# Moving sixteen modulation slabs of the first block and twelve of the last layer to other stages

## The reference, cut to what matters

```python
def ada(c, w, b):                      # first block: w_ada (1024 x 6144), for c and for c_ctx
    m = jax.nn.silu(c) @ w + b
    return split(m, 6)                 # sh1, sc1, g1, sh2, sc2, g2

u_lat = modulate(x, sh1, sc1) @ w_in   # layer norm, then * (1 + sc1) + sh1
mix   = token_mixer(u_lat, ...)        # state-space part, Fourier part, pooling part, @ w_out
x     = post_norm(x, mix, g1, ...)
x     = post_norm(x, conv_ffn(modulate(x, sh2, sc2), ...), g2, ...)

# second block, two layers, ada_w_2[layer] (1024 x 6144)
mod = silu(c) @ ada_w[layer] + ada_b[layer]          # six vectors of 1024
# layer 0: mLSTM heads and banded window attention, then a squared-ReLU MLP
# layer 1: full attention, then a squared-ReLU MLP
```

## Time and profile before

| | us |
|---|---|
| median of 3 runs | 2562.12 (2561.9 to 2563.28) |
| the profiled execution's own time | 2555.24 |
| its span | 2553.4 |
| TensorE busy | 2366.8 (93%) |
| GpSimd busy | 1061.9 (42%) |
| VectorE busy | 1166.3 (46%) |
| ScalarE busy | 792.8 (31%) |

### The profile page before, as it was taken

One profiled execution on the slowest core, in us unless ns is written; L12 is line 12 of the kernel. 1 busy time (PEld: TensorE's weight loads), 2 busy tenths in 40 slices (PEclk: granted clock), 3 DMA queues, 4 the chain that ended last, 5 costly groups with the idle time before them and its releaser, 6 DMA issues. The chain is left out here.

```text
span 2553.4 us, 35025 instructions
## 1 busy us (share of the span) xinstructions
PE 2366.8 (93%) x14323; PEld 1921.2 (75%) x14323; DVE 1166.3 (46%) x1938; ACT 792.8 (31%) x1301; POOL 1061.9 (42%) x728
## 2 busy tenths in 40 slices
PE   6987688999997999978989999999989999899999
PEld 5866466777775789866768888888867688688887
DVE  4417647856563680478345142322327752411111
ACT  4232433333334422245232111111124353322221
POOL 3326234655553332324236243443434124656553
PEclk8998898999998999979989999999989999899999
DMA  8570213544442112100113233333311101233321
GB/s 273 165 231 1 69 62 111 163 136 157 145 161 76 33 50 67 34 1 2 40 43 116 66 116 124 109 127 105 114 44 50 50 1 50 83 99 99 99 83 50
DMA packets 224701, 229.95 MB, mean 90 GB/s; under 512 B 7375, under 2 KB 221219, under 8 KB 224547
## 3 DMA queue, kind: packets, MB, share of 16 engines
q1 hardware_dynamic: 224211, 227.66, 27.7%
q10 hardware_dynamic: 336, 0.11, 0.0%
HBM read 225.65 MB, written 2.10 MB: 89 GB/s over the span
## 5 line engine op out<-in xcount | busy, mean ns | idle before, releaser
L1271 POOL TENSOR_TENSOR w_lo<-ring,w_hi 128x1024 fp32r<-128x1024 f32 x126 | 306.1, 2432 | 374.3 <-ACT w_hi L1265 374.3
L2087 DVE SCALAR_TENSOR_TENSOR xT<-ps,mods,xT 128x512 f32<-128x512 f32 (+1 forms) x160 | 108.5, 684 | 555.4 <-PE ps L1333 519.5
L1265 ACT ACTIVATE w_hi<-ring 128x1024 fp32r<-128x1024 f32 x126 | 132.7, 1057 | 537.8 <-PE ps L1333 510.4
L1331 PE MATMUL ps<-hidden_hi,w_hi 128*128 128x512 f32 (+1 forms) x768 | 273.3, 356 | 0.0
L1332 PE MATMUL ps<-hidden_lo,w_hi 128*128 128x512 f32 (+1 forms) x768 | 272.0, 354 | 0.0
L1333 PE MATMUL ps<-hidden_hi,w_lo 128*128 128x512 f32 (+1 forms) x768 | 271.6, 354 | 0.0
L2373 DVE SCALAR_TENSOR_TENSOR ffn_sums<-ps,cols,ffn_sums 128x441 f32<-128x441 f32 (+2 forms) x352 | 215.0, 687 | 105.7 <-ACT ffn_sums L2294 105.7
L1331 PE MATMUL ps<-h_hi,w_hi 128*128 128x512 f32 (+1 forms) x688 | 245.4, 357 | 1.6 <-issue 1.6
L1332 PE MATMUL ps<-h_lo,w_hi 128*128 128x512 f32 (+1 forms) x688 | 244.2, 355 | 0.0
L1333 PE MATMUL ps<-h_hi,w_lo 128*128 128x512 f32 (+1 forms) x688 | 243.8, 354 | 0.0
L2317 POOL TENSOR_TENSOR ffn_w_lo<-ring,ffn_w_hi 128x1024 fp32r<-128x1024 f32 (+2 forms) x76 | 161.6, 2128 | 194.2 <-ACT ffn_w_hi L2270 194.2
(11 more groups left out here) (446 smaller groups left out, 5294.4 us busy)
## 6 DMA issues: line engine op xcount, KB each, us to landing
ring<-in_mlp_w SPq DMA_DIRECT2D x64, 1024.0 KB, 5.4
ring<-in_ada_w SPq DMA_DIRECT2D x48, 1024.0 KB, 5.3
ring<-in_w_ada SPq DMA_DIRECT2D x24, 1024.0 KB, 9.7
ring<-in_ffn_w_up SPq DMA_DIRECT2D x22, 1024.0 KB, 7.1
ring<-in_ab_w_in SPq DMA_DIRECT2D x11, 1024.0 KB, 5.2
ring<-in_ffn_w_down SPq DMA_DIRECT2D x12, 768.0 KB, 5.5
ring<-in_w_in SPq DMA_DIRECT2D x8, 1024.0 KB, 7.4
ring<-in_c_w_in SPq DMA_DIRECT2D x6, 1024.0 KB, 5.0
```

The lines of the kernel that those rows point to most:

```text
L1265: act.activation(w_hi[m][:, 0:x["kt"], :], ring[:, x["n"] % NS, 0:x["kt"], m * P:(m + 1) * P], ACT.Copy).then_inc(SW["w_hi"].sem, 1)
L1271: pool.tensor_tensor(w_lo[m][:, 0:x["kt"], :], ring[:, x["n"] % NS, 0:x["kt"], m * P:(m + 1) * P], w_hi[m][:, 0:x["kt"], :].bitcast(F32), ...
L1331: pe.matmul(o, w_hi[m][:, k, :], h, start=(k == 0), stop=False)
L2087: return nc.vector.scalar_tensor_tensor(x, bank, column_of(gates, t * 2 + 2 * gate + r), x, ALU.mult, ALU.add)
```

## The change

In the slab list the sixteen later slabs of `w_ada` stand behind all of `w_in` instead of between them (`W["ada_late"]`), and the first twelve slabs of the second block's layer 1 stand between `ab_w_in_2` and `ab_w_out_2` (`W["ada_1"]`).

The first projection stage has no modulation slabs left but the lead's. Of the sixteen, four are done in the short stage ahead of the transposes, eight in the chunk steps (ahead of steps 1, 3, 5, 7, 10, 13, 16 and 19), and four in the gate and Fourier stage behind the sums of squares. They keep bank 6 for themselves over all these stages, so the transposes use six banks, and the pooling products go to banks 7 and 2. SyncE's queue gets loads in three stages; the `w_out` slabs are now loaded in the gate and Fourier stage, behind the Fourier matrices, instead of at the end of the projection stage. The batch ends in the gate and Fourier stage.

In the banded attention a slab stands ahead of the turning of each of the pairs 3 to 6, 9 to 12 and 15 to 18 (all narrow), in three batches of four in bank 5, which wide pairs use; so the first slab of a batch waits for the copy of the pair before, and the turning of a wide pair waits until ScalarE has copied the batch's rows. At p = 22 TensorE turns the three batches (six matmuls), and VectorE finishes behind its last pair. The split of the output weights moves from p = 12 to p = 19. In the MLP the first three quarters have four modulation slabs each (behind the w1 slabs), the fourth none.

```diff
@@ -236 +236 @@
-            add_slabs("w_ada", 0, whole, cols_of(SLAB * (8 + 2 * n), 2), 1)
+        W["ada_late"] = add_slabs("w_ada", 0, whole, cols_of(8 * SLAB, 16), 1)
         W["out"] = add_slabs("w_out", 0, whole, cols_of(0, 4), 2)
@@ -265 +265 @@
+        W["ada_1"] = add_slabs("ada_w_2", 1, whole, cols_of(0, 12), 1)
         W["ab_out"] = add_slabs("ab_w_out_2", 0, whole, cols_of(0, 4), 4)
-        W["mlp_0"], ada_col = len(stream), [0]
+        W["mlp_0"], ada_col = len(stream), [12 * SLAB]
         for q in range(4):
...
                 add_slabs("mlp_w1_2", 0, whole, [1024 * q + SLAB * j], 4)
-                add_slabs("ada_w_2", 1, whole, [ada_col[0]], 1)
-                ada_col[0] += SLAB
-            for j in range(4):
-                if q in (1, 2):
+                if q < 3:
                     add_slabs("ada_w_2", 1, whole, [ada_col[0]], 1)
                     ada_col[0] += SLAB
+            for j in range(4):
                 add_slabs("mlp_w2_2", 0, [(1024 * q, KT)], [SLAB * j], 4)
@@ -369 +368 @@
-        def transpose_pe(pe, groups):
+        def transpose_pe(pe, groups, banks=8):
...
             for u, (srcs, _) in enumerate(groups):
-                if u >= 8:
+                if u >= banks:
                     t = (tr_free_v, tr_free_a)[u % 2]
-                    pe.wait_ge(t.sem, t.at((u - 8) // 2 + 1))
+                    pe.wait_ge(t.sem, t.at((u - banks) // 2 + 1))
                 for j, s in enumerate(srcs):
...
-                    ins = pe.transpose(ps[0:f, u % 8, j * p:(j + 1) * p], s, ident[0:p, 0:p])
+                    ins = pe.transpose(ps[0:f, u % banks, j * p:(j + 1) * p], s, ident[0:p, 0:p])
@@ -719 +718 @@
-        def ada_slab(pe, which, n, batch, j, last, i=None, slabs=0):
+        def ada_slab(pe, which, n, batch, j, last, i=None, slabs=0, bank=6):
@@ -727 +726 @@
-                    ins = pe.matmul(ps[32 * q:32 * q + 32, 6, 0:SLAB], sil[:, at0:at0 + 32], ring[:, n % NS, 2 * q + kk, :],
+                    ins = pe.matmul(ps[32 * q:32 * q + 32, bank, 0:SLAB], sil[:, at0:at0 + 32], ring[:, n % NS, 2 * q + kk, :],
...
-        def ada_tiles(pe, batch, i=None):
+        def ada_tiles(pe, batch, i=None, into=(5, 0), src=None):
             turn_wait(pe, ADA["ada_rows_out"], batch + 1, i, 1)
             for m in range(2):
-                o = at(i, 64, 64 * batch + 32 * m)
-                dst = ps[:, 5, o:o + 32] if i is None else ps[:, 5, bass.ds(o, 32)]
-                ins = pe.matmul(dst, ada_rows[:, m * P:(m + 1) * P], sum_groups, start=True, stop=True)
+                o = at(i, 64, into[1] + 64 * batch + 32 * m)
+                dst = ps[:, into[0], o:o + 32] if i is None else ps[:, into[0], bass.ds(o, 32)]
+                ins = pe.matmul(dst, (ada_rows if src is None else src)[:, m * P:(m + 1) * P], sum_groups, start=True, stop=True)
             ins.then_inc(ADA["ada_tiles"].sem, 1)
...
-        def ada_take(act, n, batch, i=None, done_per_turn=0):
+        def ada_take(act, n, batch, i=None, done_per_turn=0, bank=6):
...
                 turn_wait(act, ADA["ada_tiles"], batch, i, 1)
-            act.activation(ada_rows[:, 0:SLAB], ps[:, 6, 0:SLAB], ACT.Copy).then_inc(ADA["ada_rows_out"].sem, 1)
-
-        def ada_finish(dve, lay, batches, bias_col, gain_cols):
+            act.activation(ada_rows[:, 0:SLAB], ps[:, bank, 0:SLAB], ACT.Copy).then_inc(ADA["ada_rows_out"].sem, 1)
+        def ada_finish(dve, lay, batches, bias_col, gain_cols, into=(5, 0)):
...
-                    ps[:, 5, 64 * batch:64 * batch + 64].rearrange("p (m s c) -> p s m c", m=2, c=2)[:, 0:count],
+                    ps[:, into[0], into[1] + 64 * batch:into[1] + 64 * batch + 64].rearrange("p (m s c) -> p s m c", m=2, c=2)[:, 0:count],
@@ -1690 +1689 @@
-                    (0, 0, COL["b_ada"], 8), convolve, silu_of_conv, w_low=in_w_low,
+                    None, convolve, silu_of_conv, w_low=in_w_low,
@@ -1701 +1700 @@
+        def late_ada(pe, first, last):
+            for j in range(first, last):
+                ada_slab(pe, 0, W["ada_late"] + j, 1, j, j == 15)
         with nc.Block() as block:
+            @block.sync
+            def _(sp):
+                load_slabs(sp, W["ada_late"] + 4 + NS)
+            @block.tensor
+            def _(pe):
+                late_ada(pe, 0, 4)
             @block.vector
@@ -1755 +1768 @@
             def _(pe):
-                transpose_pe(pe, groups)
+                transpose_pe(pe, groups, 6)
...
             def _(dve):
-                transpose_out(dve, groups, 0)
+                transpose_out(dve, groups, 0, 6)
...
             def _(act):
-                transpose_out(act, groups, 1)
+                transpose_out(act, groups, 1, 6)
@@ -1810 +1823 @@
         wait = lambda eng, n, v: eng.wait_ge(R[n].sem, R[n].at(v))
+        ada_at = {1: 4, 3: 5, 5: 6, 7: 7, 10: 8, 13: 9, 16: 10, 19: 11}
...
         with nc.Block() as block:
+            @block.sync
+            def _(sp):
+                load_slabs(sp, W["ada_late"] + 16)
@@ -1852 +1870 @@
+                    if s in ada_at:
+                        late_ada(pe, ada_at[s], ada_at[s] + 1)
@@ -1972 +1992 @@
+                load_slabs(sp, W["out"] + NS)
@@ -1986 +2007 @@
+                ada_take(act, W["ada_late"] + 15, 1)
@@ -2002 +2024 @@
-                    act.activation(hT[:, 6 + t, 0:LAT], ps[:, 6 + t, :], ACT.Copy, scale=sc)
+                    act.activation(hT[:, 6 + t, 0:LAT], ps[:, (7, 2)[t], :], ACT.Copy, scale=sc)
@@ -2010 +2032 @@
+                late_ada(pe, 12, 16)
                 pe.wait_ge(loaded.sem, loaded.at(16 * 11))
...
+                ada_tiles(pe, 1, None, (6, 256))
@@ -2033 +2057 @@
-                    sig(pe.matmul(ps[:, 6 + t, :], w4[:, 2 + t, :], pooled[:, t, :], start=True, stop=True), "pool")
+                    sig(pe.matmul(ps[:, (7, 2)[t], :], w4[:, 2 + t, :], pooled[:, t, :], start=True, stop=True), "pool")
@@ -2070 +2094 @@
+                ada_finish(dve, 0, [(1, 8, 16)], COL["b_ada"], None, (6, 256))
@@ -2438 +2464 @@
                         v = signals[last_w2]
-                        dve.wait_ge(mm_done, val(v, i, signals[last_w2 + 8 + 8 * (1 - layer)] - signals[last_w2] if q < 3 else 0))
+                        dve.wait_ge(mm_done, val(v, i, signals[last_w2 + 8 + 4 * (1 - layer)] - signals[last_w2] if q < 3 else 0))
                     for pos in range(m * n_r, (m + 1) * n_r):
@@ -2484 +2510 @@
                     n += 1
-                    if layer == 0:
+                    if layer == 0 and q < 3:
                         items.append(("ada", n, 1, ada_no))
...
-                    if layer == 0 and q in (1, 2):
-                        items.append(("ada", n, 1, ada_no))
-                        n, ada_no = n + 1, ada_no + 1
                     items.append(("w", n, KT, (m_hi, m_lo, 0), ranges, "dve", take, hooks))
@@ -2499 +2522 @@
             if layer == 0:
-                after = lambda dve: ada_finish(dve, 2, [(0, 0, 4), (1, 4, 8), (2, 12, 8), (3, 20, 4)], COL["b_ada2_1"], (COL["norm1_1"], COL["norm2_1"]))
+                after = lambda dve: ada_finish(dve, 2, [(0, 12, 4), (1, 16, 4), (2, 20, 4)], COL["b_ada2_1"], (COL["norm1_1"], COL["norm2_1"]))
...
             if layer == 0:
-                ada_close(4)
+                ada_close(3)
@@ -2758 +2781 @@
             wait = lambda eng, n, v: eng.wait_ge(R[n].sem, R[n].at(v))
+            def wide(n):
+                return len(blocks(n)[0]) == 5
+            narrow_runs = [[p for p in range(6 * g + 3, 6 * g + 7)] for g in range(3)]
+            assert not any(wide(pairs[p][1]) for run in narrow_runs for p in run)
+            slab_at = {p: (g, j) for g, run in enumerate(narrow_runs) for j, p in enumerate(run)}
+            lot_rows = [mean[:, g * SLAB:(g + 1) * SLAB] for g in range(3)]
+            LOT_BANK, TILES_AT = 5, (7, 256)
             with nc.Block() as block:
+                @block.sync
+                def _(sp):
+                    load_slabs(sp, W["ab_out"] + NS)
@@ -2778 +2815 @@
-                        if p == n_p // 2:
+                        if p == 19:
                             made.weights_low(pool)
@@ -2834 +2871 @@
+                        if p in slab_at:
+                            g, j = slab_at[p]
+                            if j == 0:
+                                wait(pe, "turned_a", p)
+                            ada_slab(pe, 1, W["ada_1"] + 4 * g + j, 0, j, j == 3, bank=LOT_BANK)
+                        if p == 22:
+                            wait(pe, "turned_v", p)
+                            for g in range(3):
+                                ada_tiles(pe, g, None, TILES_AT, lot_rows[g])
+                        if wide(pairs[p][1]) and p > 6:
+                            pe.wait_ge(ADA["ada_rows_out"].sem, ADA["ada_rows_out"].at(p // 6))
@@ -2887 +2935 @@
+                    ada_finish(dve, 2, [(g, 4 * g, 4) for g in range(3)], COL["b_ada2_1"], (COL["norm1_1"], COL["norm2_1"]),
```

(8 more changed lines are left out.)

6 lines of the change are left out of this document (4 added, 2 removed).

## The result

The changed kernel takes 2538.61 us (median of four executions, 2537.41 to 2541.45) against 2562.7 us before: a ratio of 0.9905 (95% interval 0.9888 to 0.9922), 24.1 us less. Forecast were 2536.4 us and a gain of 25.7.

The account below looks back on a forecast made before the run. TensorE was taken to bound the projection stage and MLP, VectorE and TensorE in tight rings the steps and attention. Terms -17.4 - 13.2 - 1.0 + 0 + 3.9 - 2.0 + 4.0 = -25.7 us gave 2536.4 us, range 2525 to 2551.

Parts of the forecast that it names:

- rival A: Whole kernel: the forecast itself, a gain of 20 to 34 us, predicted time 2536.4 us; chance 0.72.
- First projection stage, -17.4: First projection stage: seven slab pairs between units save 14.6 us, the eighth at the stage's end 2.8 us.
- rival E: Removed slabs were covered because weight split or a load ends last; only costs remain, 2568 us; chance 0.02.
- The correction by the weight-load share: Projection stage and MLP: if the missing eighth of weight-load share were slack, the -30.6 us gain becomes -26.6; not adopted.
- Short stage, 0: Short stage: four slabs fit into TensorE's 8.03 us idle time, and SyncE's loads hold its end no longer; 0.
- Early steps, 0: First eight chunk steps: slabs hidden because GpSimd works two buffers ahead; 0, bounds -1 and +6 us.
- Late steps, +3.9: Chunk steps 10, 13, 16, 19: no slack, each slab delays VectorE 0.97 us; +3.9, bounds 0 and 4.4.
- Attention, +4.0: Banded attention: groups lose 0.7, 2 and 2 us, less 1 for half clock, plus 0.3 for six turning matmuls.
- MLP, -13.2: Second block's MLP: twelve slabs removed at 1.10 us each; one batch's turning and two vector operations counted as nothing.
- B: Chunk steps and attention: tighter rings, 20 slabs cost their whole 1.10 us; gain 9.7 us, 2552.4 us; chance 0.14.
- C: Whole kernel: nearly all added slabs hidden, about 0 in the attention; 2526 us; chance 0.06.
- Rival D: Chunk steps and attention: TensorE falls to half clock, a slab costs 1.71 us; slower, 2580 us; chance 0.03.

Follow-up runs that it names:

- again: The kernel before, unchanged, profiled a second time: span 2560.7 us against 2553.4 us in its first profile.
- part one alone: Only the first block's sixteen slabs moved, attention and MLP as in the kernel before: 2549.73 us, ratio 0.9949 to the kernel before.
- part two alone: Only the second block's twelve slabs moved from MLP to attention, output weights split at pair 19, against the kernel before: 2548.56 us, ratio 0.9947.
- combined kernel: Changed kernel with SyncE's fourth load in the transposes' stage, batches turned behind pair 21's turning, split halved at pairs 17 and 18: 2529.81 us.

## Why the prediction was right, and where it was not

The mechanism stood: TensorE's time in its own stages against gaps in the others. With 2536.4 against 2538.61 us, rival A is what happened, but some terms missed and others made up for them, which is luck. Point by point, by the means of the two profiles of each kernel:

- **First projection stage, -17.4:** -17.6. The spacing was the right thing to read; no wait for the split or a load took its place, and rival E is out. The correction by the weight-load share would have cut 4 us from a gain that, with the MLP's, was in the end larger than the sum had it.
- **Short stage, 0:** +1.3. The step that failed is "SyncE's next four loads ... hold the stage's end no longer than they do". The slabs ended at 173.84, the fourth load's issue at 177.52. A stage ends when the last queue does, and SyncE's is one of them.
- **Transposes, -1.0:** nothing against the first profile of before, with the running sums -3.5 against the second, in which those two had met half clock. The bounds were too narrow for how much this moves between executions.
- **Early steps, 0:** -0.5 to -0.8 up to step 10 (bound -1). Before, half clock lay on these steps, from 5.5 to 15.7 us behind the stage's start; with the slabs it is not there.
- **Late steps, +3.9:** +1.00, +1.00, +0.90 and +1.01 us for the steps with a slab; between them 0.07 us given back in one step is taken again in the next. Together 3.9, right in mechanism and size. The stage is still 5.4 us longer, since a spell of half clock fell on steps 21 to 23 (2.0 us); it is absent in two profiles, which have 70.27 us for the stage.
- **Gate and Fourier stage, -2.0:** -1.7 in one profile, 0 in the other.
- **Attention, +4.0:** +6.1. The twelve slabs cost 3.2 us; 0.7 + 2 + 2 - 1 = 3.7 was said, and but for the 0.7 in the first group these terms came one by one (0, 2.0, 2.0, -1.0). The split's move gave 5.4 - 3.8 = 1.6 us back where 0 was taken (within the stated +-2.5). What failed is "0.3 us for six turning matmuls": in full it cost 4.4 to 4.9 us, as moving it one pair ahead showed. I priced its matmuls at full clock and did not ask what the wait ahead of it, at a place where the split stalls VectorE, would do to them and to what stands behind.
- **The attention's out projection, 0:** +1.5, its first matmuls run at half clock (0.43 us from one to the next instead of 0.23). It is so in 8 of 14 profiles, also in two whose attention has no slabs, so it does not need the slabs.
- **MLP, -13.2:** -16.5. Twelve slabs at 1.10 are 13.2, as said. Left at nothing were one batch's turning and the shorter finish (0.5 us each), and 1.6 us of idle TensorE went that no term had; 0.7 us are left over. What failed is the term "which I leave at nothing", by 1.0 us; the 1.6 us belong to a slow loop branch (last section), which no row of the prediction showed.
- **Between, 0:** +6.0 in the profiles. The changed kernel's two profiled executions were the slowest of its four each time (2541.45 and 2542.6 us), so its medians may carry less of this. The reason is open.

The attention and the short stage were forecast 3.4 us too low together, the MLP's gain 3.3 us too low, and these cancelled. Of the 7.5 us by which the profiled executions gain less than the medians (16.6 against 24.1), 6.0 are the stretch between; a near total says little about those. Rivals B and C named prices of 1.10 and about 0 for a slab in the rings; measured are 1.0 in the late steps, below 0 in the early ones (where half clock went) and 3.2 / 12 = 0.27 in the attention: neither extreme. Rival D's half clock did not come where it was priced: both rings ran at 1.00 with the slabs in them, but for the spell in steps 21 to 23.

## What to carry to other kernels

Price filler work by the engine's spacing where it is removed, and by whether a partner engine starts without a wait where it is put: that gave 17.4, 3.9 and 3.7 us where 17.6, 3.9 and 3.2 were measured. Then look at the small companions of the move: a queue that must end with the stage (SyncE's last load, 1.3 us), a batch's closing operations behind a wait at the ring's end (4.9 us), a side job beside which VectorE's operations stretch (5.4 us in one lump, 1.15 in two halves in other pairs). Put closing operations ahead of a wait that exists anyway, not behind it.

## What the runs showed of the hardware that was not expected

- Of four 1 MB loads that SyncE issued in a row as their slots came free, the issues took 0.37, 0.37, 0.81 and 3.63 us. The last of them ended 0.2 us before the first load had landed (177.52 and 177.69 us; 175.33 and 175.51 in the second profile), so a fourth issue seems to wait for a transfer ahead of it; this is inferred from the times alone. With the fourth issued in the next stage, it took 0.99 us.
- The trace's record of TensorE's branch back to the second turn of the MLP's loop is 3.57 us long in the kernel before (3.35 again, 3.87 without slabs and with the later split, 3.35 in part one alone) with 1.4 to 1.9 us of idle TensorE behind it, and 0.23 us in the changed kernel, in part two alone and in six variants. The variant with shortened late slabs has the changed MLP, loop and all, and 3.59 us (the two rows are its: the last matmul ahead of the branch and the first behind it). So the loop's content does not decide it; where it lies in TensorE's instructions may, which was not tried.

```profile
1600.99 0.28 PE L1332 MATMUL ps<-hidden_hi,w_lo 128*128 128x256 f32 x1
1602.95 0.49 PE L1330 MATMUL ps<-h_hi,w_hi 128*128 128x512 f32 x1 [1.68 <-issue]
```

- With 28 of 32 matmuls of four slabs left out, the steps were 1.8 us shorter than without a spell, yet the gate and Fourier stage behind them was 2.2 us longer than in the combined kernel, at a lower clock, and the profiled span 0.3 us longer. The price of filler work cannot be read from the whole time.
